# Layer normalisation's scaling waits tile by tile; forgetting attention's averages as two split products

## The chip, the cores and the metric

The kernel runs as one program on one core of a Trainium2 chip. What counts is the device time of a whole execution in microseconds (us), the median of several runs. The engines are named as in the profile: PE is TensorE's matrix products, PEld its weight loads, DVE is VectorE, ACT is ScalarE, POOL is GpSimd, SP is the queue that issues the stream of weights.

## What is computed

The reference is a two layer block with a second two layer stack behind it, all in float32 on 512 positions of width 1024. Two parts of it matter here.

```python
def layer_norm(x, g, b):
    mu = jnp.mean(xf, axis=-1, keepdims=True)
    var = jnp.mean(jnp.square(xf - mu), axis=-1, keepdims=True)
    return ((xf - mu) * lax.rsqrt(var + LN_EPS) * g + b)
...
def fox_attention(u, w_in, b_f, q_norm_g, k_norm_g, w_out):
    q, k, v, g, fl = jnp.split(u @ w_in, ...)
    q = rms_norm(q.reshape(bn, sn, 16, 64), q_norm_g).transpose(0, 2, 1, 3) * (64 ** -0.5)
    k = rms_norm(k.reshape(bn, sn, 16, 64), k_norm_g).transpose(0, 2, 1, 3)
    ...
    s = einsum(q, k) + f_cum[t] - f_cum[s]          # causal, blocks of 128 queries
    o = softmax(s) @ v
    return (o * jax.nn.sigmoid(g)) @ w_out
```

`rms_norm` divides by the root of the mean of squares over a head's 64 channels. Layer normalisation runs four times in the first block (numbered 0 to 3), forgetting attention once (its second layer).

## The kernel before, in words

**Layout.** Activations lie transposed: 128 channels on the partitions by 512 positions, eight such tiles for the width. A float32 product is made of three products of fp32r operands: each operand is split into a high part (a copy rounded to fp32r, by ACT) and a low part (the rest, by DVE), and PE multiplies high by high, high by low and low by high. The weights arrive from SP in panels of 128x1024 through a ring of four; `prepare` splits them on ACT (`high`, L2058) and DVE (`low`, L1285), two panels ahead of their use. Averages over channels are products with a constant matrix.

**Order.** Each engine has its own instruction list, written out by hand (`tensor_program`, `vector_program`, `scalar_program`); the engines meet at semaphores (`mark` and `at`). Nothing reorders the list: an instruction that waits holds all that stand behind it on its engine.

**Layer norms 1 to 3** (`layer_norm`, PE L780, DVE L1393, ACT L2136): the mean is in a bank of PSUM. DVE takes it off the eight tiles of the residual (L1412, "centring"), and between the third and the fourth of them makes the variance (L1410) out of a second bank that PE has filled. ACT takes the root (`inv_sqrt`, L2100 and L2103). DVE then waits for the root and for its own last centred tile, and `norm_split` scales tile by tile (L1441) and makes the low parts (L1436), with ACT making the high parts (L2165) between them. In norm 0 the variance comes only from the centred tiles. Norm 3 scales with `ln_scale` (L1429).

**Forgetting attention** (`fox`, PE L949, ACT L2349, DVE L1686) goes by head pairs hp = 0 to 7. `paired_attention` runs 34 slots; slot d = 4 hp + r works on query block 3 - r of pair hp, so that the keys read are 512, 384, 256 and 128 wide for r = 0 to 3. In a slot PE computes the scores (L918, L921), runs `fill(d, 0)`, multiplies the turned probabilities of two slots before with the values (L932), and turns those of the slot before (L947) in two halves with `fill(d, 1)` between them. DVE adds the bias and takes the maxima (L1651), runs `fill(d, 0)`, scales the probabilities (L1663, L1675), runs `fill(d, 1)` and copies turned ones (L1682). ACT takes the exponentials (L2327), runs `fill(d, 0)`, and copies turned ones (L2339).

The fills carry the next pair's projections: PE's products of the query, key and gate panels (L688 to L690), spread by `FOX_FILL`. Query and key of the next pair need a norm each, numbered z = 0 and 1. For each, ACT evicts the product (`raw`: L2072) and squares it (L2362); PE multiplies the square by `mean64` (`norm`, L957); ACT takes the root (`root`, L2100 and L2103); DVE scales (`normed`, L1699). Before, for the query (z = 0) `norm`, `root` and `normed` all stand in the second part of slot r = 1, the slot in which `raw` makes its square. For the key (z = 1), `raw` stands in r = 2 and `norm`, `root` and `normed` in the first part of r = 3, ahead of the gate's eight tiles of products on PE. The norms of pair 0 are made ahead of the slots, between two panels of the value projection.

Of the kernel before, what the change touches and what calls it, by code (L numbers as in the profile page):

```python
# [6 lines left out]
P = 128  # L7
# [343 lines left out]
def build(nc, io, table):  # L351
# [40 lines left out]
    def const(name, rows=P):  # L392
        c, w = CONST.at[name]
        return C[0:rows, c:c + w]
# [76 lines left out]
    gla_banks = lambda hp: (B[4], B[5], B[2], B[3]) if hp == 0 else (B[6], B[7], B[4], B[5])  # L471
    NF = H[0:FOX_H, 31, :]
    QG = COL[:, 80:81]
    fox_tile = lambda hp, z: H[:, 4 * (hp % 2) + z, :]

    fox_bias = lambda hd: H[:, 20 + hd % 4, :]
# [143 lines left out]
    def tensor_program():  # L620
# [329 lines left out]
        def fox():  # L950
            gemm(("fl",), u_split, ready=lambda k: ("norm_out", "ln", 1, k), idle=10)
            gemm_tok(("fv", 0), 4, 2, 512, ("fv", 0), B[4:8])

            def norm(hp, z):
                bank = gemm_bank(("fnorm", hp, z))
                pe.wait_ge(*at("fox_square", hp, z))
                ins = pe.matmul(bank[:, :], const("mean64"), H[:, 8 + 2 * z, :], start=True, stop=True)  # L957
                ins.then_inc(*mark("tensor_fox", "fox_mean", hp, z))

            def first_norms(i):  # L960
                if i == 2:
                    norm(0, 0)
                    norm(0, 1)
            gemm(("fq", 0), u_split)
            gemm(("fk", 0), u_split)
            pe.wait_ge(*at("fv_out", 0, NTB - 1))
            gemm_tok(("fv", 1), 4, 2, 512, ("fv", 1), B[4:8], first_norms)

            def begin(d):
                if d % 4 == 0:  # L970
                    pe.wait_ge(*at("fox_k", d // 4))

            def fill(d, part):

                hp, r = d // 4 + 1, d % 4
                if part == 0 and r == 3 and hp < KT:
                    norm(hp, 1)
                if part == 0 and hp < KT:
                    for name, of, a, b in FOX_FILL[r]:
                        gemm_some((name, hp + of), a, b)  # L980
                if part == 0 and hp == KT + 1 and r == 0:
                    gemm_some(("fox_out", 0), 0, 3, lambda k: ("fox_low", k))
                if part == 0 and hp == KT:
                    if r in (1, 3):
                        busy(B_of(("fg", KT - 2)), 2 if r == 1 else 1)
                    ins = gemm_some(("fg", KT - 1), 2 * r, 2 * r + 2)
                    if r < 3:
                        ins.then_inc(*mark("tensor_fox", "fox_input_free", r))
                if part == 1 and r == 1 and hp < KT:
                    norm(hp, 0)  # L990

            def out_free(d):
                if d % 4 == 0:
                    if d == 0:
                        pe.wait_ge(*at("fv_out", 1, NTB - 1))
                    if d >= 8:
                        pe.wait_ge(*at("fox_mix", d // 4 - 2))
            paired_attention(("fox",), fox_items(), FOX_PROBS, [B[4], B[5]], FOX_SLOTS, begin, fill, out_free)
# [279 lines left out]
    def vector_program():  # L1278
# [114 lines left out]
        def layer_norm(i, gcol_, bcol, mod):  # L1393
# [11 lines left out]
            if i:  # L1405
                v.wait_ge(*at("ln_rest", i))
            for k in range(KT):
                if i and k == 3:
                    v.wait_ge(*at("ln_var", i))
                    v.tensor_tensor(LN_VAR, B[3][:, :], LN_REST, ALU.subtract).then_inc(*mark("vector_norm", "ln_v", i))  # L1410
                v.wait_ge(*(at("ln_shifted", i, k) if i and k < 5 else at("res", i, k)))
                v.tensor_tensor(X[:, k, :], X[:, k, :], B[2][:, :], ALU.subtract).then_inc(  # L1412
                    *mark("vector_norm", "ln_centre", i, k))
            v.wait_ge(*at("ln_r", i))
            v.wait_ge(*at("ln_centre", i, KT - 1))
            if mod is not None:
                norm_split(("ln", i), lambda k: LNG[:, k:k + 1], lambda k: LNS[:, k:k + 1], ln_root(i))
            if i in (1, 3):
                for k in range(KT):
                    ln_scale(i, k, gcol_)  # L1420
# [265 lines left out]
        def fox():  # L1686
# [14 lines left out]
            prepare(ahead(("fv", 0, 3)))  # L1701
            prepare(ahead(("fq", 0)))
            prepare(ahead(("fk", 0)))
            prepare(ahead(("fv", 1, 1)))
            normed(0, 0)
            normed(0, 1)
# [9 lines left out]
            def fill(d, part):  # L1716
                hp, r = d // 4 + 1, d % 4
                if hp < KT:
                    if part == 0 and r != 2:
                        prepare(ahead((("fq", hp), ("fk", hp), None, ("fg", hp - 1))[r]))  # L1720
                    if (part, r) in ((1, 1), (0, 3)):
                        normed(hp, 1 - part)
                elif part == 0 and r == 0:
                    prepare(ahead(("fg", KT - 1)))
                elif hp == KT and part == 1 and r < 3:
# [323 lines left out]
    def scalar_program():  # L2049
# [299 lines left out]
        def fox():  # L2349
# [8 lines left out]
            def raw(hp, z):  # L2358
                key, tile = ("fk" if z else "fq", hp), fox_tile(hp, z)
                evict(key, tile)  # L2360
                s.wait_ge(*at("evicted", key))
                s.activation(H[:, 8 + 2 * z, :], tile, ACT.Square).then_inc(*mark(sem, "fox_square", hp, z))  # L2362

            def root(hp, z):
                s.wait_ge(*at("fox_mean", hp, z))
# [6 lines left out]
            def gate(hp):  # L2372
# [5 lines left out]
                s.activation(gt, gt, ACT.Ln, bias=1.0).then_inc(*step(sem))  # L2378
                s.wait_ge(*last(sem))
                s.activation(gt, gt, ACT.Exp, scale=-1.0).then_inc(*mark(sem, "fox_gate", hp))  # L2380
            raw(0, 0)
            raw(0, 1)
            prepare(ahead(("fv", 1, 1)))
# [3 lines left out]

            def fill(d, part):
                hp, r = d // 4 + 1, d % 4
                if part == 0 and r == 3 and hp < KT:  # L2390
                    root(hp, 1)
                if part == 0 and r == 3 and hp <= KT:
                    gate(hp - 1)
                if hp < KT:
                    if part == 0:
# [4 lines left out]
                            prepare(ahead(("fk", hp)))  # L2400
                        elif r == 2:
                            raw(hp, 1)
                    elif r == 1:
                        root(hp, 0)
                elif hp == KT and part == 0 and r < 3:
                    if r == 0:
                        prepare(ahead(("fg", KT - 1)))
# [356 lines left out]
```

## Time and profile before

| | us |
|---|---|
| Median of 3 runs | 2763.35 |
| Lowest and highest | 2762.67, 2767.46 |
| Profiled execution, its time | 2761.18 |
| Its span (first to last instruction) | 2759.7 |
| Mean granted TensorE clock | 0.996 |

The page of the profile gives an engine's busy time, its share of the span, and the number of its instructions. A row of the timeline gives start and duration in us, the engine, the line, the operation and its tiles with their shapes; "x2" says how many neighbours it merges. In brackets stands how long the engine sat idle before, and the instruction that ended this. Consecutive instructions overlap in their recorded durations, so costs are best taken as the distance from one start to the next. PEclk is the granted clock of TensorE: 1.00 is 2.4 GHz, 0.50 is 1.2 GHz.

### The profile page before, as it was taken

To read this page: it belongs to the slowest core of one execution; us is meant where nothing else is said; L and a number is where in the kernel's file an instruction comes from. 1 tells how busy PE (TensorE), PEld (TensorE's weight loads), DVE (VectorE), ACT (ScalarE), POOL (GpSimd) and SP (SyncE) were. 2 spreads that over 40 slices of the span, in tenths; PEclk is the share of its full clock that TensorE was granted. 3 is DMA by queue.
4 is the path that set the end of the run, shared out by engine and by line. 5 is a ranking of instruction groups with operands and counts; after the bars stand their busy time and mean duration, and the time that the engine had idled before them with its cause. 6 is when DMAs were issued, how large, how long until landed. Compare 5 with 4: busy or idle time off the path is not lost.

```text
span 2759.7 us, 41751 instructions
## 1 busy us (share of the span) xinstructions
PE 2664.1 (97%) x17218; PEld 2110.4 (76%) x17218; DVE 1625.9 (59%) x2919; ACT 1158.3 (42%) x2016; POOL 9.4 (0%) x21
## 2 busy tenths in 40 slices
PE   7999999999999999999998899999999988999998
PEld 6777888877666788886886668888878766788886
DVE  7887546664556865667556755444465577533334
ACT  3744334234555432424546543222355466322222
POOL 0000000000000000000000000000000000000000
PEclk9999999999999999999999999999999999999999
DMA  8364555532221465653230024444433200223322
GB/s 314 115 221 138 188 178 183 176 128 84 77 77 54 145 201 188 197 184 117 100 130 2 3 77 130 135 149 143 145 132 107 77 3 18 84 99 100 98 94 84
DMA packets 92092, 336.40 MB, mean 122 GB/s; under 512 B 10480, under 2 KB 10736, under 8 KB 91776
## 3 DMA queue, kind: packets, MB, share of 16 engines
q1 hardware_dynamic: 86656, 314.87, 34.6%
q10 hardware_dynamic: 3936, 14.64, 1.5%
q0 software_dynamic: 1312, 4.23, 0.5%
q8 instruction: 137, 2.24, 0.3%
q14 instruction: 51, 0.42, 0.0%
HBM read 331.57 MB, written 2.13 MB: 121 GB/s over the span
## 4 chain that ended last, share of the span: by engine, by line
PE 85%; DVE 8%; ACT 6%; issue 2%; DMA 0%; DVEq 0%; SPq 0%; ACTq 0%
PE bank L669 22%; PE bank L671 22%; PE bank L670 22%; PE bank L688 1%; PE bank L689 1%; PE bank L690 1%; PE bank L947 1%; PE bank L932 1%; ACT probs L2327 1%; PE bank L918 1%; PE bank L730 1%; PE bank L731 1%; PE bank L732 1%; PE bank L712 1%; PE bank L714 1%
## 5 line engine op out<-in xcount | busy, mean ns | idle before, releaser
L1285 DVE TENSOR_TENSOR weights_low<-weight_ring,weights_high 128x1024 fp32r<-128x1024 f32 x404 | 494.1, 1224 | 429.6 <-ACT weights_high L2058 429.1
L669 PE MATMUL bank<-in_high,weights_high 128*128 128x512 f32 x1800 | 706.8, 393 | 3.9 <-DVE in_low L1436 2.8
L671 PE MATMUL bank<-in_high,weights_low 128*128 128x512 f32 x1800 | 701.2, 390 | 0.0
L670 PE MATMUL bank<-in_low,weights_high 128*128 128x512 f32 x1800 | 701.1, 389 | 0.0
L2058 ACT ACTIVATE weights_high<-weight_ring 128x1024 fp32r<-128x1024 f32 x404 | 424.8, 1052 | 409.8 <-PE bank L671 310.1
L669 PEld LDWEIGHTS bank<-in_high,weights_high 128*128 128x128 f32 x1800 | 338.2, 188 | 79.0 <-DVE in_low L1436 5.1
L671 PEld LDWEIGHTS bank<-in_high,weights_low 128*128 128x128 f32 x1800 | 338.2, 188 | 71.2
L670 PEld LDWEIGHTS bank<-in_low,weights_high 128*128 128x128 f32 x1800 | 338.4, 188 | 69.6 <-issue 0.7
L669 PE MATMUL bank<-hidden_split,weights_high 128*128 128x512 f32 x896 | 349.5, 390 | 0.0
L670 PE MATMUL bank<-hidden_split,weights_high 128*128 128x512 f32 x896 | 348.6, 389 | 0.0
L671 PE MATMUL bank<-hidden_split,weights_low 128*128 128x512 f32 x896 | 348.6, 389 | 0.0
L1294 DVE CUSTOM_DVE_ANT_0 weight_ring<-weight_ring,silu_c,vectors 128x1024 f32<-128x1024 f32 x192 | 244.5, 1279 | 0.1
L669 PEld LDWEIGHTS bank<-hidden_split,weights_high 128*128 128x128 f32 x896 | 168.2, 188 | 35.6 <-issue 0.5
L670 PEld LDWEIGHTS bank<-hidden_split,weights_high 128*128 128x128 f32 x896 | 168.2, 188 | 35.2 <-issue 0.5
L671 PEld LDWEIGHTS bank<-hidden_split,weights_low 128*128 128x128 f32 x896 | 168.2, 188 | 35.1
L2175 ACT ACTIVATE hidden_split<-tmp 128x512 fp32r<-128x512 f32 x108 | 68.3, 632 | 269.2 <-DVE tmp L1844 200.7
L2072 ACT ACTIVATE tmp<-bank 128x512 f32<-128x512 f32 x68 | 40.7, 598 | 221.5 <-PE bank L671 219.0
L1459 DVE TENSOR_TENSOR hidden_split<-tmp,hidden_split 128x512 fp32r<-128x512 f32 x108 | 74.8, 693 | 75.4 <-ACT hidden_split L2175 75.4
L1346 DVE SCALAR_TENSOR_TENSOR residual<-bank,modulations,residual 128x512 f32<-128x512 f32 x64 | 48.0, 750 | 119.3 <-PE bank L671 119.2
L2327 ACT ACTIVATE probs<-probs,columns 128x256 f32<-128x256 f32 (+4 forms) x144 | 73.7, 513 | 91.9 <-DVE columns L1651 90.1
L2072 ACT ACTIVATE tmp<-bank,vectors 128x512 f32<-128x512 f32 (+1 forms) x65 | 44.7, 688 | 135.2 <-PE bank L671 125.9
L1844 DVE TENSOR_TENSOR tmp<-bank,tmp 128x512 f32<-128x512 f32 x44 | 30.4, 692 | 113.6 <-PE bank L671 113.6
(395 smaller groups left out, 3345.9 us busy)
## 6 DMA issues: line engine op xcount, KB each, us to landing
weight_ring<-stream SPq DMA_DIRECT2D x596, 512.0 KB, 3.4
mixer_out<-cmp ACTq DMA_DIRECT2D x6, 1024.0 KB, 4.9
hidden<-forget_rows POOLq DMA_DIRECT2D x16, 256.0 KB, 3.8
residual<-x ACTq DMA_DIRECT2D x4, 512.0 KB, 8.3
mixer_out<-cmp SPq DMA_DIRECT2D x2, 1024.0 KB, 6.5
out<-mixer_out ACTq DMA_DIRECT2D x4, 512.0 KB, 2.7
constants<-consts ACTq DMA_DIRECT2D x1, 1821.5 KB, 9.8
silu_c<-c ACTq DMA_DIRECT2D x2, 512.0 KB, 4.4
```

The lines of the kernel that those rows point to most:

```text
L669: pe.matmul(bank[:, :], WHI[:, z, cols], high, start=(k == 0), stop=False)
L670: pe.matmul(bank[:, :], WHI[:, z, cols], low, start=False, stop=False)
L671: ins = pe.matmul(bank[:, :], WLO[:, z, cols], high, start=False, stop=(k == ktiles - 1))
L1285: v.tensor_tensor(WLO[:, z, :], ring[:, n % RING, :], WHI[:, z, :].bitcast(F32), ALU.subtract).then_inc(*mark("weights_low", "low", n))
L1294: v.tensor_tensor_reduce(w, w, SC[:, :], 1.0, vec1("ada_b", col, col + 1), ALU.mult, ALU.add, MODS[:, col:col + 1]).then_inc(*mark("modula ...
L1346: v.scalar_tensor_tensor(X[:, m, :], B_of(key)[:, :], gcol_[:, m:m + 1], X[:, m, :], ALU.mult, ALU.add).then_inc(*mark("residual", "evicte ...
L1459: v.tensor_tensor(HSPLIT[:, 1, at_, :], tmp, HSPLIT[:, 0, at_, :].bitcast(F32), ALU.subtract).then_inc(*mark("vector_mlp", *event))
L1844: v.tensor_tensor(tmp, B_of(("gup", l, j))[:, :], tmp, ALU.mult).then_inc(*mark("vector_mlp", "evicted", ("gup", l, j)))
L2058: s.activation(WHI[:, i % NSPLIT, :], ring[:, n % RING, :], ACT.Copy).then_inc(*mark("weights_high", "high", n))
L2072: s.activation(dst, view(B_of(key)[:, :]), func, **kw).then_inc(*mark("scalar_evict", "evicted", key))
L2175: s.activation(HSPLIT[:, 0, at_, :], tmp, ACT.Copy).then_inc(*mark("scalar_mlp", *event))
L2327: s.activation(p, p, ACT.Exp, bias=nm, scale=-1.0, accum_out=COL[:, c + 2 + z:c + 3 + z]).then_inc(*mark(sem, *name, "exp", i))
```

## The change

In layer normalisation, DVE no longer waits for its last centred tile before the scaling (norms 0, 1, 2); instead each scaling waits for its own tile. The variance is subtracted behind the second centred tile, not the third (norms 1, 2, 3).

In forgetting attention the square is split like any other operand. ACT squares the evicted tile twice, once to float32 and once to fp32r (`fox_high`); DVE subtracts (`square_low`) and writes the low part. PE multiplies each by `FOX_MEAN`, an fp32r copy of `mean64` that ACT makes once. The steps also move: the query's `norm`, `root` and `normed` go from the second part of slot r = 1 to the first part of r = 2. There `root` stands ahead of the key's `raw` on ACT, and `norm` ahead of the last four tiles of the key's products on PE. The query's `square_low` stands ahead of the panel's low part on DVE in r = 1, the key's in the second part of r = 2. The key's `norm`, `root` and `normed` stay where they were.

```diff
+    fox_squares = lambda z: H[:, 8 + 2 * z, :]
+    fox_high, fox_low = (lambda z: HSPLIT[:, 1, 9 + z, :]), (lambda z: HSPLIT[:, 1, 11 + z, :])
+    FOX_MEAN = HSPLIT[:, 1, 13, 0:P]
...
             def norm(hp, z):
                 bank = gemm_bank(("fnorm", hp, z))
-                pe.wait_ge(*at("fox_square", hp, z))
-                ins = pe.matmul(bank[:, :], const("mean64"), H[:, 8 + 2 * z, :], start=True, stop=True)
+                pe.wait_ge(*at("fox_mean_split"))
+                pe.wait_ge(*at("fox_square_low", hp, z))
+                pe.matmul(bank[:, :], FOX_MEAN, fox_high(z), start=True, stop=False)
+                ins = pe.matmul(bank[:, :], FOX_MEAN, fox_low(z), start=False, stop=True)
...
                 hp, r = d // 4 + 1, d % 4
-                if part == 0 and r == 3 and hp < KT:
-                    norm(hp, 1)
+                if part == 0 and r > 1 and hp < KT:
+                    norm(hp, r - 2)
...
-                if part == 1 and r == 1 and hp < KT:
-                    norm(hp, 0)
...
             for k in range(KT):
-                if i and k == 3:
+                if i and k == 2:
                     v.wait_ge(*at("ln_var", i))
...
             v.wait_ge(*at("ln_r", i))
-            v.wait_ge(*at("ln_centre", i, KT - 1))
             if mod is not None:
-                norm_split(("ln", i), lambda k: LNG[:, k:k + 1], lambda k: LNS[:, k:k + 1], ln_root(i))
+                norm_split(("ln", i), lambda k: LNG[:, k:k + 1], lambda k: LNS[:, k:k + 1], ln_root(i), ("ln_centre", i))
+            else:
+                v.wait_ge(*at("ln_centre", i, KT - 1))
...
+            def square_low(hp, z):
+                v.wait_ge(*at("fox_square", hp, z))
+                v.tensor_tensor(fox_low(z), fox_squares(z), fox_high(z).bitcast(F32), ALU.subtract).then_inc(
+                    *mark(sem, "fox_square_low", hp, z))
...
                 if hp < KT:
+                    if part == 0 and r == 1:
+                        square_low(hp, 0)
                     if part == 0 and r != 2:
                         prepare(ahead((("fq", hp), ("fk", hp), None, ("fg", hp - 1))[r]))
-                    if (part, r) in ((1, 1), (0, 3)):
-                        normed(hp, 1 - part)
+                    if part == 0 and r > 1:
+                        normed(hp, r - 2)
+                    if part == 1 and r == 2:
+                        square_low(hp, 1)
...
-                s.activation(H[:, 8 + 2 * z, :], tile, ACT.Square).then_inc(*mark(sem, "fox_square", hp, z))
+                s.activation(fox_squares(z), tile, ACT.Square).then_inc(*step(sem))
+                s.activation(fox_high(z), tile, ACT.Square).then_inc(*mark(sem, "fox_square", hp, z))
...
+            s.activation(FOX_MEAN, const("mean64"), ACT.Copy).then_inc(*mark(sem, "fox_mean_split"))
...
-                if part == 0 and r == 3 and hp < KT:
-                    root(hp, 1)
+                if part == 0 and r > 1 and hp < KT:
+                    root(hp, r - 2)
...
-                    elif r == 1:
-                        root(hp, 0)
```

## Rows read from the trace of the kernel before

**Rows 1.** page, parts 1 and 4: busy time by engine; chain by engine.

```profile
PE 2664.1 (97%) x17218; PEld 2110.4 (76%) x17218; DVE 1625.9 (59%) x2919; ACT 1158.3 (42%) x2016; POOL 9.4 (0%) x21
...
PE 85%; DVE 8%; ACT 6%; issue 2%; DMA 0%; DVEq 0%; SPq 0%; ACTq 0%
```

**Rows 2.** windows: stretch, us, busy of PE, PEld, DVE, ACT, POOL, PEclk, DMA, GB/s.

```profile
700.00:740.00 40.00, 39.57 (x239) 26.99 (x237) 22.43 (x64) 23.42 (x50) 1.07 (x2) 1.00 0.22 67
```

**Rows 3.** source L957, then waits 632 to 880: us, times, longest.

```profile
L957 PE MATMUL bank<-hidden,constants x32: 590/592/667, 633.8 to 832.1; 128*128 128x512 f32 x32
...
PE bank L957 <- ACT hidden L2362: 2.6, 6, 0.4
```

**Rows 4.** timeline, PE, one head pair: start, us, operation, idle before.

```profile
712.56 1.02 PE L957 MATMUL bank<-hidden,constants 128*128 128x512 f32 x2
...
713.96 0.43 PE L918 MATMUL bank<-hidden 64*64 64x256 f32 x2
...
720.22 1.10 PE L957 MATMUL bank<-hidden,constants 128*128 128x512 f32 x2 [0.43 <-ACT hidden L2362]
...
721.39 0.40 PE L689 MATMUL bank<-in_low,weights_high 128*128 128x512 f32 x1
...
721.62 0.39 PE L690 MATMUL bank<-in_high,weights_low 128*128 128x512 f32 x1
...
728.11 0.65 PE L918 MATMUL bank<-hidden 64*64 64x512 f32 x2
```

**Rows 5.** timeline, ACT, the same head pair.

```profile
710.88 0.63 ACT L2362 ACTIVATE hidden<-hidden 128x512 f32<-128x512 f32 x1
...
711.42 1.04 ACT L2058 ACTIVATE weights_high<-weight_ring 128x1024 fp32r<-128x1024 f32 x1
...
717.66 0.51 ACT L2327 ACTIVATE probs<-probs,columns 128x256 f32<-128x256 f32 x1 [2.69 <-DVE columns L1651]
...
718.84 0.58 ACT L2072 ACTIVATE hidden<-bank 128x512 f32<-128x512 f32 x1
...
719.45 0.63 ACT L2362 ACTIVATE hidden<-hidden 128x512 f32<-128x512 f32 x1
...
721.76 0.67 ACT L2100 ACTIVATE hidden<-bank,constants 128x512 f32<-128x512 f32 x1
...
723.00 1.04 ACT L2058 ACTIVATE weights_high<-weight_ring 128x1024 fp32r<-128x1024 f32 x1
```

**Rows 6.** timeline, DVE, the same head pair.

```profile
712.50 1.22 DVE L1285 TENSOR_TENSOR weights_low<-weight_ring,weights_high 128x1024 fp32r<-128x1024 f32 x1 [2.87 <-ACT weights_high L2058]
...
715.01 0.75 DVE L1699 SCALAR_TENSOR_TENSOR hidden<-hidden,columns 128x512 f32<-128x512 f32 x1 [0.43 <-ACT hidden L2103]
...
717.20 0.42 DVE L1651 CUSTOM_DVE_ANT_0 probs<-bank,hidden 128x256 f32<-128x256 f32 x1
...
725.21 0.75 DVE L1699 SCALAR_TENSOR_TENSOR hidden<-hidden,vectors 128x512 f32<-128x512 f32 x1
```

**Rows 7.** timeline, PE, the first head pair's second average.

```profile
664.55 1.10 PE L957 MATMUL bank<-hidden,constants 128*128 128x512 f32 x2
```

**Rows 8.** timeline, layer norm behind the first MLP, DVE and ACT.

```profile
574.83 3.07 DVE L1412 TENSOR_TENSOR residual<-residual,bank 128x512 f32<-128x512 f32 x5
...
575.70 0.63 ACT L2103 ACTIVATE tmp<-tmp 128x512 f32<-128x512 f32 x1
...
578.00 1.41 DVE L1441 SCALAR_TENSOR_TENSOR hidden<-residual,columns,tmp 128x512 f32<-128x512 f32 x2
```

**Rows 9.** windows and timeline (PE): where the clock fell or stayed.

```profile
125.00:135.00 10.00, 7.28 (x145) 6.56 (x145) 9.82 (x16) 5.64 (x8) 0.00 (x0) 0.83 0.36 114
...
1475.00:1485.00 10.00, 8.86 (x166) 6.58 (x166) 8.34 (x27) 5.88 (x21) 0.00 (x0) 0.66 0.01 2
...
820.00:860.00 40.00, 36.46 (x245) 24.60 (x244) 26.62 (x80) 24.09 (x55) 0.00 (x0) 1.00 0.13 42
...
1475.02 0.69 PE L1170 MATMUL bank<-constants,work 64*64 64x64 f32 x32 [1.42 <-DVE work L1958]
```

More of the change, by code:

```diff
@@ L1703, in fox @@
             prepare(ahead(("fk", 0)))
+            def square_low(hp, z):
+                v.wait_ge(*at("fox_square", hp, z))
+                v.tensor_tensor(fox_low(z), fox_squares(z), fox_high(z).bitcast(F32), ALU.subtract).then_inc(
+                    *mark(sem, "fox_square_low", hp, z))
+            square_low(0, 0)
+            square_low(0, 1)
             prepare(ahead(("fv", 1, 1)))
```

## Prediction

> **What bounds the kernel now.** I read the page first: the share of each engine, and the chain that ended last. PE is busy for 97% of the span and has 85% of the chain [rows 1], so a microsecond counts when PE loses or gains it. The change touches two places: the norms, some 20 us each, and forgetting attention from 633 to 860 us. There the windows show PE busy for 39.57 of 40 us at the full clock, while DVE and ACT have 22.43 and 23.42 us [rows 2]. An averaged reading says: PE is the bound, the other two have room, so less work for PE is a gain. That is true of the sum and not of the order, so I read the three timelines of one head pair side by side.
>
> PE runs without a gap through the pair's 28 us but for one place: it waits 0.43 us for the key's average (L957 at 720.22), because ACT's square of the key (L2362) is only just done. In the waits this shows as 2.6 us over six times [rows 3, 4]. It is the one place in the pair where the chain through ACT is already as late as PE. The change lengthens just this chain.
>
> **PE's own work.** The 16 averages are 32 recorded passes [rows 3]. Two passes of one average start 0.43 us apart (1.02 for both less 0.59 for the last), so an average holds PE for 0.86 us [rows 3, 4]. An fp32r product of the same shape takes 0.23 us from start to start, 721.39 to 721.62 [rows 4]; two of them are 0.45 us. So 0.41 us is saved per average. For the two averages of pair 0, ahead of the slots, no wait is shown before, and between the squares and the averages stand two panels of products for the values, which is more than one more square and one subtraction. There the saving stands: -0.8 us.
>
> **The chain of the key's average, pairs 2 to 7.** I follow it from DVE's maxima of slot r = 2 to PE, with the time of the traced pair.
>
> 1. In slot r = 1 ACT's second square stands ahead of the high half of a panel. A square and what follows it start 0.54 us apart, 710.88 to 711.42 [rows 5], so that the panel's high half, and DVE's low half behind it (712.50), come 0.54 us later. DVE's new `square_low` for the query lies in the 2.87 us for which DVE is idle there [rows 6] and costs nothing (if it had no such cover, 0.6 us).
> 2. DVE loses the query's `normed` from slot r = 1: 0.67 us of its own (0.75 long [rows 6], less the 0.08 by which neighbours overlap, 0.68 long at 0.60 apart [rows 8]), and 0.51 us that it waited for ACT before it (0.43 shown as idle at 715.01 [rows 6], and the overlap). With the 0.54 us of step 1 the maxima of r = 2 (717.20 [rows 6]) come 0.64 us earlier, and so do ACT's exponentials, which waited for them (717.66, idle 2.69 us [rows 5]). This I take in full; the scores are ready, as PE comes earlier by the 0.86 us of the average that has left slot r = 1.
> 3. ACT now takes the query's root before it evicts the key. Root costs 1.24 us, from 721.76 to 723.00 [rows 5]: +1.24. Then evicting and one square as before, and the second square, +0.54.
> 4. The low part on DVE behind it: 0.04 us to start and 0.68 us to run, by the centring of the norm, of the same form and size: (3.07 - 0.68)/4 = 0.60 apart and 0.68 long [rows 8]. +0.72. DVE is free by then: the query's `normed` waits for the root, but ends about 0.3 us before the second square does.
>
> The sum is 1.24 + 0.54 + 0.72 - 0.64 = 1.86 us: the key's average starts 1.86 us later than at 720.22. It is then 0.41 us shorter, so the gate's products, all of slot r = 3 and the next pair are **1.45 us later**. PE meanwhile has less in front of it: it arrives 0.86 us earlier for the query's average that has gone from r = 1 and 0.45 us later for the one that is now in r = 2, so at 719.38 and not 719.79. Its idle time grows from 0.43 to 2.7 us. What is saved on PE is thus eaten before it shows: it only lengthens the wait. Six pairs give +8.7 us.
>
> In pair 1 there was no idle time before `normed` and no wait at PE (664.55 [rows 7]). Only 0.67 - 0.54 = 0.13 us is regained: 1.24 + 0.54 + 0.72 - 0.13 - 0.41 = **+2.0 us**.
>
> **What is late next.** DVE's low part also stands ahead of the turned copy and the maxima of slot r = 3, so I estimate that ACT's and DVE's work there shifts by 2.2 us, PE's by 1.45. The scaled key was ready at 725.96 for scores at 728.11 [rows 4, 6]: 2.15 us of slack, of which 0.7 is used. It isn't late. The query's average has its low part at 712.09 + 0.68 = 712.8, before the scores of r = 2 even start (713.96 - 0.86 = 713.1 [rows 4]). The order of the banks stays. SP's stream and POOL's bias rows lose nothing: they hang on the same steps, a little later, with the same work before them.
>
> **Layer norm.** DVE waits for its last centred tile to be written. Centring starts at 574.83 with a pitch of 0.60 and ends at 577.90; the scaling starts at 578.00, and without the drain it could start 0.60 us behind the last centring, at 577.82 [rows 8]. That is 0.18 us in each of norms 1 and 2, in which DVE sets the pace; norm 0 waits for its root, norm 3 keeps the wait: -0.4 us. The eight new waits are met before they are reached. Moving the variance brings nothing: the root ends at 576.33 (575.70 + 0.63) and DVE centres until 577.90 [rows 8], so that a root 0.6 us earlier waits too. What a variance asked for too early could cost is not in the trace; it is bounded by the one place that it moves, 0.6 us in three norms, and I take 0. The Trainium skill speaks against a gain here: "VectorE: DVE Perf Modes", section "The DRAIN you can't avoid", says that the next operation doesn't start until the pipe is empty and that a semaphore in between costs nothing extra. By it this part would bring 0 and not 0.4 us; the row disagrees, with recorded starts 0.60 apart and operations 0.68 long [rows 8].
>
> **The clock.** The sum so far is 8.7 + 2.0 - 0.8 - 0.4 = +9.5 us. But 2.7 us without products is more than the trace shows anywhere here. At the end of this attention PE was idle for 3.54 of 40 us, in several short gaps, and the clock stayed at 1.00 (820 to 860). In the second stack a gap of 1.42 us ahead of 1475.02, between small products, was followed by half clock: a mean of 0.66 over 1475 to 1485, which is 10 x 0.34/0.5 = 6.8 us at 1.2 GHz; and from 125 to 135, where PE was idle for 2.72 us, it was 0.83, which is 3.4 us [rows 9]. The new gap stands behind small products too (values, turning, scores of width 128), so I expect the clock to fall in most pairs. I take the shorter stretch, as the gate's 24 dense products follow: 3.4 us at half clock lose 1.7 us each. With six falls of seven that is **+10.2 us**; the bounds are 0 (no fall) and 23.8 (seven times 6.8/2).
>
> **How the numbers follow.** +9.5 + 10.2 = +19.7 us on the profiled execution's 2761.18, which is 2780.9. The median of the runs lies 2.2 us above the profiled one, so the forecast is **2783**. A measurement can tell about 0.2%, 5.5 us.
>
> - Chain late and clock falls in most pairs, as above: 2778 to 2789. Chance 0.62.
> - Rival A, chain late and the clock stays (or falls once or twice): 2763 + 9.5 = 2773, up to 2776. The row of 820 to 860 speaks for it, the one at 1475 against. 0.24.
> - Rival B, on the other side: the chain is covered and PE keeps its saving. The price is 16 x 0.41 = 6.6, the old waits of 2.6 and the norm's 0.4, so 2754. The mechanism is VectorE releasing the maxima of r = 2 earlier than in my step 2. It decides from 2.9 us earlier (1.24 + 0.54 + 0.72 and 0.43 of new lead on PE's side), against the 0.64 that I find. For it speaks that ACT is idle for 2.69 us ahead of those exponentials; against it, that DVE has to run the panel's low half and the probabilities first. 0.06.
> - Rival C, half of this: a chain that is late by about the saving of an average, within 5 us of before. 0.04.
> - Rival D, each fall lasts 6.8 us: 2763 + 9.5 + 23.8 = 2797. 0.04.
>
> The change does what it says, as its parts are there in the diff; that the norm's part has an effect too small to see is in all of these. The range 2770 to 2789 takes in the first two cases and leaves out B, C and D. Faster 0.06, same 0.04, slower 0.90.
>
> **What would show it.** The waits of PE at the average, for DVE's low part: seven, of about 2.7 us, some 19 us in all, and none at the query's. ACT's root in slot r = 2 between exponentials and key. PE passes of the average 0.23 us apart. The distance of two pairs 29.3 us where the clock stays, some 31 where it falls, against 27.8. PEclk below 1.00 in windows behind the waits; this is the weakest step. If the exponentials of r = 2 start 2 us or more earlier against PE's scores, step 2 is wrong, and with it the sign.

## The result and the profile after

| | before | after |
|---|---|---|
| Median of 4 runs each, measured together (us) | 2765.26 | 2782.64 |
| Lowest and highest | 2762.67, 2767.46 | 2780.13, 2787.43 |
| Profiled execution | 2761.18 | 2784.57 |
| Its span | 2759.7 | 2783.1 |
| Mean granted clock in it | 0.996 | 0.989 |

The ratio on record, 1.0071 [1.0059, 1.0083], is not the quotient of these two medians: it stands for some 20 us (16 to 23), while the medians lie 17.4 us apart (1.0063). Later measurements of before had medians of 2762.3 to 2763.2, 19 to 20 us below that of after. So the change costs 17 to 20 us. The forecast was 2783, slower.

Of the executions reported below one, of the first kernel with the key's average among the gate's products, was slow (4430.7 us at a granted clock of 0.556) and is left out.

The page of after, parts 1 and 4, against [rows 1]: PE, DVE and ACT are all busier in sum, and PE's share of the chain falls from 85 to 83%.

```profile
PE 2675.0 (96%) x17218; PEld 2123.9 (76%) x17218; DVE 1636.5 (59%) x2935; ACT 1164.9 (42%) x2033; POOL 9.4 (0%) x21
...
PE 83%; DVE 8%; ACT 6%; issue 2%; DMA 0%; DVEq 0%; SPq 0%; ACTq 0%
```

Work was taken from PE, yet it is busy for 11 us more, a first sign of the clock: at half clock an fp32r product of 128x512 is recorded 0.63 us long (728.59) and not 0.39 (720.02). PE's waits in after, 632 to 880 us, against [rows 3]:

```profile
PE bank L961 <- DVE hidden_split L1710: 18.8, 7, 2.7
```

One wait per pair, all at the key's average and for its low part; none at the query's. The windows of after (columns as in [rows 2]): all of the attention, the stretch of [rows 2], and the 10 us behind one of the seven waits.

```profile
633.00:860.00 227.00, 208.19 (x1221) 150.33 (x1223) 125.11 (x338) 124.71 (x260) 6.43 (x12) 0.95 0.21 68
...
700.00:740.00 40.00, 37.32 (x220) 26.57 (x220) 22.17 (x60) 21.16 (x44) 1.07 (x2) 0.95 0.22 75
...
727.00:737.00 10.00, 9.65 (x50) 7.19 (x50) 4.54 (x15) 4.89 (x10) 1.07 (x2) 0.83 0.31 107
```

A mean clock of 0.83 over 10 us is 10 x 0.17/0.5 = 3.4 us at 1.2 GHz. The windows behind the other six waits show the same. I call such a stretch a fall. Now the chain itself, in the pair that answers to [rows 4 to 6]. PE:

```profile
705.57 0.65 PE L921 MATMUL bank<-hidden 64*64 64x512 f32 x2
...
718.39 0.43 PE L921 MATMUL bank<-hidden 64*64 64x256 f32 x2
...
718.98 0.50 PE L961 MATMUL bank<-hidden_split 128*128 128x512 f32 x1
719.32 0.39 PE L962 MATMUL bank<-hidden_split 128*128 128x512 f32 x1
...
727.35 0.47 PE L961 MATMUL bank<-hidden_split 128*128 128x512 f32 x1 [2.68 <-DVE hidden_split L1710]
727.65 0.40 PE L962 MATMUL bank<-hidden_split 128*128 128x512 f32 x1
...
736.47 0.65 PE L921 MATMUL bank<-hidden 64*64 64x512 f32 x2
```

ACT, from the exponentials of r = 2 to the key's second square (the root is at 723.48, the key's eviction at 724.72):

```profile
722.30 0.51 ACT L2341 ACTIVATE probs<-probs,columns 128x256 f32<-128x256 f32 x1 [3.54 <-DVE columns L1654]
...
723.48 0.67 ACT L2114 ACTIVATE hidden<-bank,constants 128x512 f32<-128x512 f32 x1
...
724.72 0.58 ACT L2086 ACTIVATE hidden<-bank 128x512 f32<-128x512 f32 x1
725.33 0.63 ACT L2376 ACTIVATE hidden<-hidden 128x512 f32<-128x512 f32 x1
725.86 0.61 ACT L2377 ACTIVATE hidden_split<-hidden 128x512 fp32r<-128x512 f32 x1
```

DVE, the maxima of r = 2 and the two steps around the key's low part:

```profile
721.83 0.42 DVE L1654 CUSTOM_DVE_ANT_0 probs<-bank,hidden 128x256 f32<-128x256 f32 x1
...
724.84 0.75 DVE L1702 SCALAR_TENSOR_TENSOR hidden<-hidden,columns 128x512 f32<-128x512 f32 x1 [1.91 <-ACT hidden L2117]
...
726.51 0.69 DVE L1710 TENSOR_TENSOR hidden_split<-hidden,hidden_split 128x512 fp32r<-128x512 f32 x1 [0.19 <-ACT hidden_split L2377]
```

Counted from the scores of r = 2, the key's average starts 727.35 - 718.39 = 8.96 us later; before it was 720.22 - 713.96 = 6.26 [rows 4]. Those scores come 0.86 us earlier in the pair than before, so the average is 8.96 - 6.26 - 0.86 = 1.84 us late, of 1.86 forecast. The pair lasts 736.47 - 705.57 = 30.90 us. Before it was 728.11 - 700.27 = 27.84, from the row in [rows 4] and this one:

```profile
700.27 0.65 PE L918 MATMUL bank<-hidden 64*64 64x512 f32 x2
```

The seven distances from one pair to the next are 27.84 us before but for the first, 25.91, and 30.87 after but for the first, 29.45.

From the first scores of pair 0 to those of pair 7 the profiled execution lost 21.7 us: 3.5 in the first of the seven distances (29.45 - 25.91) and 3.0 in each of the other six. Ahead of it 1.3 us were gained. Some 3 us more were lost behind it, in the second stack, where the mean clock differs from one execution to the next (0.99 over 1460 to 1700 us in before, 0.96 in after, and 0.96 to 1.00 in the others here). I put no cause of the change to these 3 us.

### The profile page after: what moved, and what is told of

The parts are those of the page before. It is cut to its first block, busy times and chain, and to the rows that moved or that the text cites. A ratio compares the mean times of both kernels' runs of the same rounds, so it can differ in the third digit from the quotient of the medians.

```text
span 2783.1 us, 41784 instructions
## 1 busy us (share of the span) xinstructions
PE 2675.0 (96%) x17218; PEld 2123.9 (76%) x17218; DVE 1636.5 (59%) x2935; ACT 1164.9 (42%) x2033; POOL 9.4 (0%) x21
## 4 chain that ended last, share of the span: by engine, by line
PE 83%; DVE 8%; ACT 6%; issue 2%; DMA 0%; DVEq 0%; SPq 0%; ACTq 0%
PE bank L672 22%; PE bank L673 21%; PE bank L674 21%; PE bank L950 1%; PE bank L935 1%; PE bank L691 1%; PE bank L921 1%; PE bank L692 1%; PE bank L693 1%; PE bank L733 1%; PE bank L734 1%; PE bank L735 1%; DVE weights_low L1287 1%; ACT probs L2341 1%; PE bank L715 1%
```

## The experiments

Theory T is that of the prediction: the chain of the key's average is late by the order on ACT and DVE, and the wait that it makes on PE brings the clock down. Its rivals are that the price lies in the split itself, in the norm's part or in the moves alone. The experiments first take the parts one by one, then the clock, then the order. Where the distance of two pairs is given, it is read from one first scores row (128 by 512 keys, L918 or L921) to the next.

### The norm's part alone

Against before:

```diff
-                if i and k == 3:
+                if i and k == 2:
                     v.wait_ge(*at("ln_var", i))
...
             v.wait_ge(*at("ln_r", i))
-            v.wait_ge(*at("ln_centre", i, KT - 1))
             if mod is not None:
-                norm_split(("ln", i), lambda k: LNG[:, k:k + 1], lambda k: LNS[:, k:k + 1], ln_root(i))
+                norm_split(("ln", i), lambda k: LNG[:, k:k + 1], lambda k: LNS[:, k:k + 1], ln_root(i), ("ln_centre", i))
+            else:
+                v.wait_ge(*at("ln_centre", i, KT - 1))
```

> Only the layer norm's part of the change. Theory (the loss is all in the attention): the time stays within 0.1% of before, as the part is worth 0.4 us; in the trace the scaling of norm 1 starts 0.60 us behind the last centring's start where it was 0.78, and the clock in 633 to 860 stays at 1.00. Rival (the earlier variance or the eight waits hold DVE up and cost part of the 19 us): slower by 2 us or more.

Measured: 2762.5 against 2762.3, ratio 1.0001 [0.9991, 1.0011]; pairs 27.84 us, as before. DVE in this kernel, the centring behind the variance and the scaling:

```profile
573.72 3.67 DVE L1412 TENSOR_TENSOR residual<-residual,bank 128x512 f32<-128x512 f32 x6
...
577.31 1.41 DVE L1442 SCALAR_TENSOR_TENSOR hidden<-residual,columns,tmp 128x512 f32<-128x512 f32 x2
```

The last centring starts at 573.72 + 5 x 0.60 = 576.7, and the scaling 0.60 us behind it. Before, it was 578.00 - (574.83 + 4 x 0.60) = 0.78 us [rows 8]. So the wait for its own last tile cost DVE 0.18 us, in two norms 0.4 us: there in the rows, and too small for the medians. The interval leaves at most 3 us to the norm's part; it doesn't carry the loss.

### The moves alone, with the float32 average

Against before; ACT's roots and PE's averages move in the same way:

```diff
-                if part == 0 and r == 3 and hp < KT:
-                    norm(hp, 1)
+                if part == 0 and r > 1 and hp < KT:
+                    norm(hp, r - 2)
...
-                    if (part, r) in ((1, 1), (0, 3)):
-                        normed(hp, 1 - part)
+                    if part == 0 and r > 1:
+                        normed(hp, r - 2)
...
-                if part == 0 and r == 3 and hp < KT:
-                    root(hp, 1)
+                if part == 0 and r > 1 and hp < KT:
+                    root(hp, r - 2)
```

> Before, with the query's average, root and scaling moved to slot r = 2 as in the change, but the old float32 average and the old layer norm. Theory (a sum of terms on the key's chain): the root adds 1.24 us, the scaling that leaves slot r = 1 gives back 0.51 + 0.67 us, so the key's average starts only 0.06 us later; PE idles 0.5 us there as before, the clock stays at 1.00, and the time is that of before, +1 us. Rival (the place of the root ahead of the key is what costs, whatever stands behind it): PE idles 1.7 us or more at the key's average and the time is at least 8 us above before.

Measured: 2765.7 against 2762.3, ratio 1.0007 [0.9998, 1.0017]; pairs 27.90 us. PE's waits and the key's average:

```profile
PE bank L957 <- ACT hidden L2360: 3.7, 7, 0.6
...
749.69 1.10 PE L957 MATMUL bank<-hidden,constants 128*128 128x512 f32 x2 [0.52 <-ACT hidden L2360]
```

The root ahead of the key costs 1.24, the scaling that leaves r = 1 gives 0.67 + 0.51 = 1.18 back: +0.06 per pair, as measured (27.90 - 27.84). The moves alone are within 0.2%, and their rival, 8 us or more, is out.

### The split alone, at the old places

Against after:

```diff
-                if part == 0 and r > 1 and hp < KT:
-                    norm(hp, r - 2)
+                if part == 0 and r == 3 and hp < KT:
+                    norm(hp, 1)
...
+                if part == 1 and r == 1 and hp < KT:
+                    norm(hp, 0)
...
-                    if part == 0 and r > 1:
-                        normed(hp, r - 2)
+                    if (part, r) in ((1, 1), (0, 3)):
+                        normed(hp, 1 - part)
...
-                if part == 0 and r > 1 and hp < KT:
-                    root(hp, r - 2)
+                if part == 0 and r == 3 and hp < KT:
+                    root(hp, 1)
...
+                    elif r == 1:
+                        root(hp, 0)
```

> The change with its layer norm and its split averages, but with the query's average, root and scaling in slot r = 1 where they were. Theory: the key's chain gets the second square and the low part, 0.54 + 0.72 us, and nothing back; PE idles 1.7 us at the key's average, a pair is 0.9 us longer, in all +5 us without a fall of the clock and up to +16 us if it falls in every pair (what a gap of 1.7 us does to the clock is open). Rival (the split itself is cheap, and only the moves cost): within 2 us of before or faster.

Measured: 2775.6 against 2762.3, ratio 1.0044 [1.0029, 1.0059]. PE's waits (both averages now), the key's average of one pair, the whole attention, and DVE's scaling of the query in r = 1:

```profile
PE bank L961 <- DVE hidden_split L1712: 13.0, 14, 1.7
...
754.38 0.47 PE L961 MATMUL bank<-hidden_split 128*128 128x512 f32 x1 [1.70 <-DVE hidden_split L1712]
...
633.00:860.00 227.00, 212.85 (x1271) 150.86 (x1269) 131.58 (x353) 130.11 (x269) 6.43 (x12) 0.98 0.22 73
...
747.92 0.75 DVE L1704 SCALAR_TENSOR_TENSOR hidden<-hidden,columns 128x512 f32<-128x512 f32 x1
```

A pair lasts 28.68 us where the clock stayed at 1.00 (+0.84), 30.3 where it fell. It fell behind three of the seven waits: never behind the first, which was 1.06 us long, and behind three of the six of 1.65 to 1.70 us. The seven distances together are 11.4 us longer than before: 1.4 in the first, 3 x 0.84 and 3 x 2.48 in the others. The split alone loses time in spite of PE's shorter average: second square and low part are 0.54 + 0.72 = 1.26 us on the key's chain, 0.41 of it comes back.

The parts don't add up: 0.06 + 0.84 = 0.90 us per pair, while both together cost 1.42 (next run). The missing half microsecond is, by the rows, one wait of DVE. Before, DVE idles 0.43 us ahead of the query's scaling in r = 1 (0.51 with the 0.08 by which neighbours overlap) [rows 6]. Here that idle time is gone (the row at 747.92 shows none): the query's second square, 0.54 us, has been absorbed in it. The moves alone gain it by taking the scaling away. Both together can have it once only.

### After, with the clock held up

PE computes products of constants into the bank of the average while it would wait; they change no result. At first six (`busy(bank, 6)`), then three:

```diff
             def norm(hp, z):
                 bank = gemm_bank(("fnorm", hp, z))
+                if hp and z:
+                    busy(bank, 3)
                 pe.wait_ge(*at("fox_mean_split"))
```

> The changed kernel with six products of 384 columns on constants ahead of the key's average on PE, 2.0 us in the 2.7 us for which PE waits there (pairs 1 to 7); they write the average's own bank before it does and change no result. Theory (half of the loss is the clock): no granted clock below 1.00 from 633 to 860, a pair takes 29.3 us and not 30.9, and the time is 11 us below the changed kernel's, +9 us on before. Rival (the fall of the clock costs little, the loss lies in waits alone): the time is that of the changed kernel, +17 us on before, or more by what the fillers delay.

Measured: 2782.9, ratio 1.0071 [1.0055, 1.0087]; pairs 31.15 us; clock 1.00 from 633 to 860.

```profile
756.35 4.14 PE L643 MATMUL bank<-constants 128*128 128x384 f32 x12 [0.68 <-ACT hidden L2088]
760.03 0.69 PE L963 MATMUL bank<-hidden_split 128*128 128x512 f32 x1
```

I had mis-sized them, and the 11 us of gain that I expected did not come. A float32 product of 384 columns is two recorded passes of some 0.33 us, so that six hold PE for about 4 us, past the low part. The run keeps the clock up and gives the gain back in fillers; it decides nothing by its time. So with half of them:

> The changed kernel with three products of 384 columns on constants ahead of the key's average, where the kernel with six held PE for 4.0 us (twelve passes of 0.33 us), longer than the wait of 2.7 us that it was to fill, and so paid with the clock what it lost in passes. Three are six passes, 2.0 us, behind 0.7 us of waiting for the bank. Theory (the clock is half of the loss): clock 1.00 from 633 to 860, a pair takes 29.3 to 29.4 us, the time is 9 to 11 us below the changed kernel's, +8 to +10 us on before. Rival (the fall of the clock costs nothing that shows): within 3 us of the changed kernel's 17 to 20 us.

Measured: 2772.3 against 2763.2, ratio 1.0033 [1.0019, 1.0047]. The attention's window, the fillers with the average behind them, and two first scores:

```profile
633.00:860.00 227.00, 221.03 (x1320) 155.84 (x1318) 132.25 (x356) 129.96 (x271) 6.45 (x12) 1.00 0.22 73
...
733.26 0.65 PE L921 MATMUL bank<-hidden 64*64 64x512 f32 x2
...
753.04 2.20 PE L643 MATMUL bank<-constants 128*128 128x384 f32 x6 [0.68 <-ACT hidden L2088]
755.04 0.47 PE L963 MATMUL bank<-hidden_split 128*128 128x512 f32 x1
...
762.51 0.65 PE L921 MATMUL bank<-hidden 64*64 64x512 f32 x2
```

The clock is 1.00 and the pair 762.51 - 733.26 = 29.25 us (29.3 forecast); pair 1 is 1.93 us longer than before (2.0 forecast). The average starts 21.78 us behind the pair's first scores (755.04 - 733.26), as in after (727.35 - 705.57), so the fillers cost nothing. What is left is the chain, 29.26 - 27.84 = +1.42 per pair. The fall costs 30.87 - 29.26 = 1.61, and seven of them 11.3 us: the larger half of the loss. The medians agree, though the two were not measured together: 2782.6 - 2772.3 = 10.3, and the ratios to before differ by 0.38%, 10.5 us.

### The root and the scaling of the query behind the key

Against after:

```diff
-                    if part == 0 and r > 1:
-                        normed(hp, r - 2)
+                    if part == 0 and r == 3:
+                        normed(hp, 1)
                     if part == 1 and r == 2:
                         square_low(hp, 1)
+                        normed(hp, 0)
...
-                if part == 0 and r > 1 and hp < KT:
-                    root(hp, r - 2)
+                if part == 0 and r == 3 and hp < KT:
+                    root(hp, 1)
...
                             raw(hp, 1)
+                            root(hp, 0)
```

> The changed kernel, with ACT evicting and squaring the key ahead of the query's root in slot r = 2, and DVE scaling the query behind the key's low part. Theory: this takes the root's 1.24 us out of the chain; PE idles 1.4 to 1.5 us at the key's average and not 2.7, a pair takes 28.1 us, the time is before +1 us, and up to +6 if the clock falls in some pairs as it did in the kernel with the old places. Rival (the wait is owed to the second square and the low part alone): PE still idles 2.5 us or more, +15 us or more.

Measured: 2763.4 against 2763.2, ratio 0.9996 [0.9986, 1.0006]; pairs 28.00 us; clock 1.00 over the attention.

```profile
PE bank L961 <- DVE hidden_split L1710: 10.2, 7, 1.5
...
747.85 0.47 PE L961 MATMUL bank<-hidden_split 128*128 128x512 f32 x1 [1.44 <-DVE hidden_split L1710]
```

The wait shrinks by 2.68 - 1.44 = 1.24 us, just the root. The pair is 30.87 - 28.00 = 2.87 us shorter: 1.24 of the wait and 1.61 of the fall, within 0.02. With the same operations, the same split and the same amount of work, the loss is gone within the interval: 1.24 us of order took all falls of the clock with it. This is the run that tells T from "the split is dear".

### The key's average among the gate's products

Against after: PE takes five of the gate's eight tiles first.

```diff
-                if part == 0 and r > 1 and hp < KT:
-                    norm(hp, r - 2)
-                if part == 0 and hp < KT:
+                if part == 0 and r == 2 and hp < KT:
+                    norm(hp, 0)
+                if part == 0 and r == 3 and hp < KT:
+                    gemm_some(("fg", hp - 1), 0, 5)
+                    norm(hp, 1)
+                    gemm_some(("fg", hp - 1), 5, 8)
+                elif part == 0 and hp < KT:
...
-                        busy(B_of(("fg", KT - 2)), 2 if r == 1 else 1)
+                        busy(B_of(("fnorm", KT - 1, 1)), 2 if r == 1 else 1)
```

> The changed kernel, with PE making the key's average behind five of the gate's eight tiles and not ahead of them. Theory: PE no longer waits for the low part, no fall of the clock; but the scaled key is late next, because DVE makes a panel's low part ahead of it: PE waits 1.3 to 1.5 us for it at the scores of slot r = 0, and the time is within 3 us of before. Rival (the key has slack enough, 2.15 us in the trace of before): no such wait, 9 us below before.

Measured: 2762.4 (median of nine) against 2763.2, ratio 1.0003 [0.9990, 1.0015]; pairs 28.24 us; clock 1.00 over the attention. PE's waits and one of the scores:

```profile
PE bank L921 <- DVE hidden L1706: 6.2, 7, 0.9
PE bank L691 <- ACT hidden L2090: 4.8, 7, 0.7
...
757.40 0.65 PE L921 MATMUL bank<-hidden 64*64 64x512 f32 x2 [0.88 <-DVE hidden L1706]
```

The wait at the average is gone, and two new ones stand in its place. The scores of the next pair wait 0.88 us for the scaled key (1.3 to 1.5 forecast), since its average now comes late and DVE makes a panel's low half before it scales. The gate's first product waits 0.68 us for the bank that ACT's eviction of the key frees, because the gate now takes the bank that the average had; this one I had not foreseen.

On the next kernel DVE scales before it makes that low half, and nothing else differs:

```diff
-                    if part == 0 and r != 2:
-                        prepare(ahead((("fq", hp), ("fk", hp), None, ("fg", hp - 1))[r]))
                     if part == 0 and r > 1:
                         normed(hp, r - 2)
+                    if part == 0 and r != 2:
+                        prepare(ahead((("fq", hp), ("fk", hp), None, ("fg", hp - 1))[r]))
```

> As the kernel before it, with DVE scaling the key ahead of the panel's low part in slot r = 3. Theory: nothing waits, the saving on PE shows in full: 16 x 0.41 of the averages, 2.6 us of the old wait and 0.4 us of the layer norm, 9.5 us below before, 2753; a pair takes 26.6 us. Rival (DVE or ACT become the bound as their order tightens): PE waits a microsecond or more per pair somewhere else and the gain is below 3 us.

Measured: 2759.0 against 2763.2, ratio 0.9983 [0.9971, 0.9996]; pairs 27.28 us, where I had forecast 26.6. The gain is 4 us where I had forecast 9.5. The wait of the scores is gone; the other has stayed, and its 0.68 us is the difference of the two pairs:

```profile
745.67 0.50 PE L691 MATMUL bank<-in_high,weights_high 128*128 128x512 f32 x1 [0.68 <-ACT hidden L2090]
```

### Both orders together, with the split and without

The last kernel, and the root and scaling of the query behind the key; this also lets ACT evict the key 1.24 us earlier, and so frees the bank. Against after, beside PE's edit above:

```diff
+                    if part == 0 and r == 3:
+                        normed(hp, 1)
                     if part == 0 and r != 2:
                         prepare(ahead((("fq", hp), ("fk", hp), None, ("fg", hp - 1))[r]))
-                    if part == 0 and r > 1:
-                        normed(hp, r - 2)
                     if part == 1 and r == 2:
                         square_low(hp, 1)
+                        normed(hp, 0)
...
                             raw(hp, 1)
+                            root(hp, 0)
```

> Both re-orderings at once: ACT takes the key ahead of the query's root, PE makes the key's average behind five of the gate's eight tiles, DVE scales the key ahead of the panel's low part and the query behind the key's low part. In the kernel with only the latter part PE still waited 0.7 us per pair for the bank that ACT's eviction of the key sets free. Theory: that eviction now comes 1.24 us earlier, this wait goes too, a pair takes 26.6 us against 27.8, and the time is 9 us below before (2754). Rival (the rest of the wait moves to another bank or to the scores): a pair of 27.2 us or more, 4 us below before, as in the kernel without the second re-ordering.

Measured: **2755.3 against 2762.6, ratio 0.9969 [0.9959, 0.9980]**: 0.3% faster than before, and so faster than both kernels of this case. Two first scores, and the average among the gate's products:

```profile
723.22 0.65 PE L921 MATMUL bank<-hidden 64*64 64x512 f32 x2
...
745.77 0.39 PE L961 MATMUL bank<-hidden_split 128*128 128x512 f32 x1
746.00 0.39 PE L962 MATMUL bank<-hidden_split 128*128 128x512 f32 x1
...
749.75 0.65 PE L921 MATMUL bank<-hidden 64*64 64x512 f32 x2
```

The pair is 26.53 us, and no wait is left at an average or at a gate's bank. Then the same order with the float32 average of before: `norm` waits for `fox_square` and multiplies by `mean64`, the second square and `square_low` are left out.

```diff
-                pe.matmul(bank[:, :], FOX_MEAN, fox_high(z), start=True, stop=False)
-                ins = pe.matmul(bank[:, :], FOX_MEAN, fox_low(z), start=False, stop=True)
+                ins = pe.matmul(bank[:, :], const("mean64"), fox_squares(z), start=True, stop=True)
...
-                s.activation(fox_squares(z), tile, ACT.Square).then_inc(*step(sem))
-                s.activation(fox_high(z), tile, ACT.Square).then_inc(*mark(sem, "fox_square", hp, z))
+                s.activation(fox_squares(z), tile, ACT.Square).then_inc(*mark(sem, "fox_square", hp, z))
```

> The same order, but with the float32 average of before: no second square, no low part. Theory (16 x 0.41 us is what the split is worth once nothing waits): a pair takes 27.4 us, 3 us below before and 6 us above the split one. Rival (the order is worth the gain, the split nothing): within 2 us of the split one.

Measured: 2760.1 against 2762.6, ratio 0.9991 [0.9981, 1.0001]; pairs 27.40 us. The order alone takes away the old wait of 0.43 us (27.84 - 27.40 = 0.44); in the median this doesn't stand out from the noise. And where the chain is covered, the split is worth 27.40 - 26.53 = 0.87 us per pair (2 x 0.41 = 0.82 by the prediction's figures), 4.8 us in the medians of the two kernels, of 6 forecast. The same edit that costs 0.84 us per pair at the old places gains 0.87 here.

## Why the prediction was right, point by point

| Step | forecast | measured |
|---|---|---|
| Root ahead of the key's eviction | +1.24 | 1.24 (723.48 to 724.72) |
| Second square | +0.54 | 0.53 (725.33 to 725.86) |
| Low part on DVE and the way to PE | +0.72 | 0.04 + 0.69 = 0.73 (square's end 726.47, start 726.51, end 727.20) |
| Maxima of r = 2 earlier | -0.64 | -0.66 (below) |
| Key's average later | +1.86 | +1.84 |
| PE's wait there | 2.7, seven, 19 in all | 2.68 (2.75 in pair 1), seven, 18.8 |
| Pairs 2 to 7 without a fall | +1.45 each | +1.42 |
| Pair 1 without a fall | +2.0 | +1.93 |
| One fall | +1.7, six of seven | +1.61, seven of seven |
| Ahead of the first scores (pair 0, norms) | -1.2 | -1.27 (first scores at 646.52, then 645.25), in part luck (below) |

**The maxima.** They stand 721.83 - 718.39 = 3.44 us behind PE's scores, before 717.20 - 713.96 = 3.24 [rows 4, 6]; with scores 0.86 us earlier that is 0.66 us earlier. This was the step on which the sign hung: the scaling's leaving gives 1.18 and the query's second square takes 0.54 of it. Rival B, with its full gain, would have needed more than the 2.9 that the prediction names: with maxima 0.64 earlier its own sum leaves a wait of 2.7, so the wait is gone only at 2.7 + 0.64 = 3.3. It left out the 0.41 us by which PE comes earlier. At 0.66 measured this changes nothing. Rival C, a loss of about one average's saving, has no place beside an average that is 1.84 us late.

**PE's saving.** The passes of an average start 0.34 and 0.30 us apart in after, where it follows small products or a wait. The 0.23 that the prediction named as a sign shows only between large products, as in the combined kernel. The average still holds PE for 0.54 to 0.57 us (718.98 to 719.55, 727.35 to 727.89), less than the 0.86 before. In after PE came to the key's average earlier, as forecast, and stood there for longer. The combined kernels show that the saving was there all the time.

**The clock** was called the weakest step. It held, with the count one too low and the price a little too high: 6 x 1.7 = 10.2 forecast, 7 x 1.61 = 11.3 measured. Rival A, the same chain and no fall, is what the kernel with three fillers runs: 2772.3, where A said 2773. Rival D fell, as each fall lasted 3.4 us and not 6.8. One reading behind this step was wrong: a gap of 2.7 us is not more than the trace of before shows. What the prediction took as 2.72 us of idle PE from 125 to 135 is the end of a single gap of 4.25 us, behind full-size products and ahead of small ones:

```profile
127.72 1.98 PE L880 MATMUL bank<-hidden 64*64 64x64 f32 x64 [4.25 <-DVE hidden L1587]
```

Ahead of this gap the clock was 1.00 (115 to 125), and behind it stood just the 3.4 us at half clock that the prediction chose. The forecast of a fall rested on better ground than it says; that all seven waits would bring one was not to be had from it.

**The norms.** The rows of norm 1 (0.78 to 0.60 us) bear out 0.18 us, and norm 2 has the same distances. The Trainium skill ("VectorE: DVE Perf Modes", "The DRAIN you can't avoid") has a semaphore cost nothing, as the next operation waits for an empty pipe anyway; by this alone the distance would not have changed. The same section adds that a next operation starts earlier where it is not held, that is, not made to wait until all those ahead of it are done; with this the rows agree, as the centrings are 0.68 us long and 0.60 apart. They don't agree with a wait that costs nothing: here it costs 0.18 us, which no median can tell.

**Ahead of the first scores.** From the first pass of pair 0's averages to the second product behind them PE took 635.73 - 633.78 = 1.95 us before and 634.50 - 633.37 = 1.13 after, which bears out the -0.8. That the whole came out at -1.27 is in part luck: five kernels with the same code up to there (after, the two with fillers, the split at the old places, the key first) reached these scores at 644.53 to 646.90 us, a spread larger than the term.

**The sum** of the measured terms, 6 x 1.42 + 1.93 + 11.3 - 1.27 = +20.5 us, lies above the difference of the two medians, +17.4, and below that of the profiled executions, +23.4; the ratio's interval, 16 to 23 us, holds it. That the median met the forecast to within 1 us is closer than the steps deserve: the clock's term was 1.1 us too small, and both medians move by a few microseconds from one set of runs to another. What the clock does in the second stack differs too, and I can't assign the rest.

## What to carry to other kernels

Before an engine that is the bound is relieved, look for the place where it already waits, however short: what is saved ahead of that place only lengthens the wait, and what the saving adds to the chain that ends there is paid, as far as no other idle time on that chain takes it up. The lever is then the order on the helpers (the wanted chain ahead of the unwanted one, here 1.24 us) and ready work ahead of the consumer on the bound engine. Edits that live on the same slack don't add up: measured each alone they cost 0.06 and 0.84 us, together 1.42.

## What I had not expected of the hardware

- How the clock takes gaps of PE behind the same small products of a slot: 2.67 to 2.75 us was followed by half clock in seven of seven cases, 1.65 to 1.70 us in three of six, 1.43 to 1.51 us (the root behind the key) in none of seven. In before a gap of 1.42 us in the second stack was followed by a fall (PEclk 0.66) [rows 9]; the same gap ahead of the same products some 730 us later was not (timeline, then window):

```profile
2206.41 0.69 PE L1170 MATMUL bank<-constants,work 64*64 64x64 f32 x32 [1.42 <-DVE work L1958]
...
2206.00:2216.00 10.00, 6.78 (x166) 4.73 (x166) 8.80 (x29) 5.74 (x21) 0.00 (x0) 1.00 0.02 3
```

  So the length of the gap alone doesn't decide. What does was not tried. Each fall in the attention lasted about 3.4 us and cost 1.6.
- Seven short fillings of 2 us, products whose result nobody reads, brought the clock to 1.00 and 10 us back. A float32 product of 384 columns is two passes of some 0.33 us.
- A wait can sit in the rotation of the banks: moving one product by five tiles gave the gate the bank that the key still held, 0.68 us in each pair.
